# Regrouped adaLN panels, a later input load, moved context steps and paired heads in a two-model kernel on one core

## The chip, the core and the metric

The kernel runs on one core of a Trainium2 chip, in one launch. The metric is the device time of the whole program in microseconds (us). All data is fp32; a fp32 matmul appears in the trace as two TensorE records.

## What is computed

Two small models are chained on 256 tokens of width 1024. The first has two blocks with adaptive layer norm (adaLN), each with a mixture of 32 experts; the second has two layers with a second stream of 256 context tokens, whose input does not depend on the first model. Cut to what matters:

```python
for l in range(2):                                    # first model
    sh1, sc1, g1, sh2, sc2, g2 = split(silu(c) @ w_ada[l] + b_ada[l])
    u = x * (1 + sc1) + sh1
    mix = even_mixer(u) if l == 0 else odd_mixer(u)   # 0: stick-breaking (8 heads of 64) and retention
    x = layer_norm(alpha * x + (1 + g1) * mix)        # 1: differential attention
    u = x * (1 + sc2) + sh2
    x = layer_norm(alpha * x + (1 + g2) * moe(u))     # 32 experts, 2 per token:
                                                      # (silu(xb @ w1[e]) * (xb @ w3[e])) @ w2[e]
h, hc = x, ctx                                        # second model; its adaLN is of c_2 and c_ctx_2
for i in range(2):
    a, ac = modulate(h, ...), modulate(hc, ...)
    y, yc = swa(a, ac) if i == 0 else neighborhood(a, ac)  # 16 heads of 64, keys: own and context
    h = h + gt1 * y;  h = h + gt2 * swiglu(modulate(h, ...))
    if i == 0:
        hc = hc + gt1c * yc;  hc = hc + gt2c * swiglu(modulate(hc, ...))
```

In the first layer of the second model, query heads share four key and value heads; its scores are masked to a window, those of the second layer have a bias table per head. Every query also sees all 256 context keys.

## The kernel before, in words

**Weights and the ring.** The run is one pass over some 670 MB of weights. Nearly all come in loads of 1 MB (1024 KB, 1.0486 MB) through `ring`, 12 slots in SBUF. Python code (L430 to 590) writes the order of the work by hand with `job(...)`, `ada_jobs(...)`, `ctx_jobs(...)` and `expert_jobs(...)`; the same calls append to `loads`. SyncE's queue runs through `loads` in that order (the loop at L744): load n waits until load n-12, the one that had its slot, is released, and so does everything behind it. A load is released by the TensorE tile that read it last; a load for context steps by the last of the steps that share it (`clast`), an expert load by the end of its phase. Expert loads (issued at L695) pick their expert from a table that the routing computes at run time, so the first of a layer waits for the routing (`info_done`), and all that stand behind it wait too.

**Start and even mixer (TensorE at L950).** ScalarE's own DMA queue issues, one behind the other, `cols`, `const` (0.86 MB by its shape), `x` and `first` (tables of the first mixer; 1 MB each) at L1708. The adaLN weights of the four conditionings are panels of two loads each (`ada(L, g0, g1)`, 16 records a panel, 1.9 us), 12 panels to a layer; the first four are needed before `x` can be modulated into `u`. Then seven projections even.0 to even.6 follow (14 us each, two loads each; two of them in another orientation), with one adaLN panel behind each and from even.3 on two, and the rest of the panels between the parts of the stick-breaking and retention heads. The output projection out0.0 ends the stage.

**Context steps.** All work of the context stream is cut into steps (`context_steps`, L105): q, k, v projections, heads, output, gate, up, down, and keys and values of the second layer. A projection step has 16 records and takes some 3.5 us of TensorE. A 1 MB load serves two such steps (gate n and gate n+1 share one, q and k likewise; a down load serves two down steps). `CTX_PLAN` and `MOE_PLAN` (L75) say how many steps stand at which point of the main stream: after a layer norm (`ln0a`, `ln0b`), in the routing (`route0a`, `route0b`), and in an expert pass at nine places, "g" (after the gather), after the phases 0 to 3, "t" (after the transposes), after phases 4 and 5, and "s" (after the scatter):

```python
CTX_PLAN = {"even": 2, "ln0a": 2, "route0a": 2, "route0b": 3, "ln0b": 2, "ln1a": 2, "route1a": 2, "route1b": 3}
MOE_PLAN = (("111212111",) * 6 + ("211000000",),
            ("111111111", "000101010", "111111111", "000101010", "111111111", "000101010", "111111111", "332000000"))
```

TensorE, ScalarE and VectorE each run their part of a step where `ctx(point)` stands in their own program.

**Experts (TensorE at L1139).** A pass takes four experts (24 loads) or, in three passes of layer 1, one or two (6 or 12 loads): a gather of token blocks by matmul (32 records), four phases gate and up, two phases down with four loads each, a scatter. Layer 0 has seven passes and one left-over pass or more, whose experts are read at run time; layer 1 has eight passes and left-over ones.

**Attention of the second model (TensorE at L1246, VectorE at L2312).** Iteration n makes the scores of head n for both query halves (tiles aS), the transposes of the probabilities of head n-2 (aT), and every second n the output product of a pair (aO). Head n lies in partitions 0 to 63 or 64 to 127 by its parity, and so do the operands of its score products, 64 rows of the array:

```python
d, kv = n % 2, n // 4
at = slice(64 * d, 64 * d + 64)
for qb in range(2):
    one_tile(T(f"aS{L}.{n}", qb), lambda o: [
        (o[:, 0:S], q[:, P * qb:P * qb + P], own),
        (o[:, S:2 * S], q[:, P * qb:P * qb + P], far)])
```

VectorE subtracts the row maxima (`shift`) and scales by the sums (`norm`), ScalarE takes the exponentials and moves the transposes. `SEQ` (L593) is the order of (head, half).

## Time and profile before

| | |
|---|---|
| median of 3 runs | 2567.42 us (2562.49 to 2575.24) |
| profiled execution, its own time | 2564.78 us |
| its span | 2563.0 us |
| TensorE (PE) busy | 2256.5 us, 88% of the span |
| VectorE (DVE) busy | 753.7 us, 29% |
| ScalarE (ACT) busy | 456.2 us, 18% |
| mean granted clock of TensorE | 0.947 of full |
| DMA moved | 675.08 MB, mean 263 GB/s |

The page cuts the span into 40 equal slices of 64 us. A digit is a tenth, 9 being 90% or more:

```profile
PE   5987897898997599888989898679999999889999
...
DVE  1136245322111114561112231147510013761000
...
PEclk9999989999998899899999999888999999899999
DMA  9799379999999946439797999941133443203430
GB/s 398 312 389 366 148 293 421 394 422 415 422 421 412 421 171 250 177 153 421 293 422 294 388 384 404 421 174 66 38 131 140 164 148 126 90 20 131 164 115 17
```

The first four slices are the start and the even mixer, slices 6 to 14 the first expert layer, 15 to 17 the odd mixer, 18 to 26 the second expert layer, and the rest the second model. Where the DMA row stands at 9 and more, the weights come as fast as the queue brings them; from slice 27 on they come faster than they are used. TensorE's digit is high nearly everywhere, also where the transfers set the pace, because its instructions are spread over the stage; so neither row alone says what ends a stage.

### The profile page before, as it was taken

How to read it: one execution, taken by the hardware profiler on the slowest of the kernel's cores; microseconds unless marked ns; L12 is line 12 of the kernel's file. 1: busy time of each engine (PE TensorE's matmuls, PEld its weight loads, DVE VectorE, ACT ScalarE, POOL GpSimd, SP SyncE). 2: the span in 40 equal slices, each digit the busy share in tenths (PEclk: the TensorE clock that was granted, in tenths of full speed). 3: DMA queues.
4: the chain of work that ended last, by engine and by line, in shares of the span. 5: the costliest groups of instructions: out<-in, count | busy, mean ns of one | idle time of the engine just before them, and what ended most of it. 6: DMA issues, size and time to landing. Idle time of an engine off the chain costs nothing.

```text
span 2563.0 us, 29352 instructions
## 1 busy us (share of the span) xinstructions
PE 2256.5 (88%) x11792; PEld 1578.4 (62%) x11792; DVE 753.7 (29%) x1897; ACT 456.2 (18%) x1141; POOL 27.8 (1%) x43
## 2 busy tenths in 40 slices
PE   5987897898997599888989898679999999889999
PEld 3654763455664284675555454257688888568888
DVE  1136245322111114561112231147510013761000
ACT  1012113312000022120000221034510011441000
POOL 0000000000000000000000000000000000110000
PEclk9999989999998899899999999888999999899999
DMA  9799379999999946439797999941133443203430
GB/s 398 312 389 366 148 293 421 394 422 415 422 421 412 421 171 250 177 153 421 293 422 294 388 384 404 421 174 66 38 131 140 164 148 126 90 20 131 164 115 17
DMA packets 94052, 675.08 MB, mean 263 GB/s; under 512 B 10832, under 2 KB 10992, under 8 KB 12384
## 3 DMA queue, kind: packets, MB, share of 16 engines
q1 hardware_dynamic: 91296, 664.84, 64.0%
q0 software_dynamic: 2048, 5.21, 0.8%
q10 hardware_dynamic: 576, 3.17, 0.3%
q8 instruction: 95, 1.56, 0.2%
q14 instruction: 37, 0.30, 0.0%
HBM read 672.13 MB, written 1.05 MB: 263 GB/s over the span
## 4 chain that ended last, share of the span: by engine, by line
PE 69%; DMA 16%; DVE 10%; ACT 2%; issue 2%; SPq 1%; DVEq 0%; ACTq 0%
PE bank L763 68%; DMA ring<-in_moe_w 14%; DMA ring<-in_w_ada 1%; DVE work L2335 1%; DMA ring<-in_even_w_out 1%; DVE tiny L2323 1%; DVE work L1860 1%; DVE scratch L1860 1%; ACT work L1384 1%; DVE work L2346 1%; PE bank L1269 1%; ACT u L1384 1%; ACT res L1384 1%; ACT scratch L1384 0%; SPq L695 0%
## 5 line engine op out<-in xcount | busy, mean ns | idle before, releaser
L763 PE MATMUL bank<-u,ring 128*128 128x256 f32 x2912 | 651.6, 386 | 33.7 <-ACT u L1384 22.1
L763 PEld LDWEIGHTS bank<-u,ring 128*128 128x128 f32 x2912 | 562.8, 194 | 122.2 <-issue 32.7
L763 PE MATMUL bank<-ring,work 128*32 128x512 f32 (+2 forms) x2880 | 411.2, 658 | 117.3 <-DMA ring<-in_moe_w 105.5
L763 PEld LDWEIGHTS bank<-ring,work 128*32 128x32 f32 (+2 forms) x2880 | 119.6, 123 | 363.8 <-issue 358.8
L763 PE MATMUL bank<-scratch,ring 128*128 128x256 f32 x1120 | 256.3, 383 | 0.3 <-issue 0.3
L1384 ACT ACTIVATE work<-bank 128x256 f32<-128x256 f32 (+2 forms) x144 | 70.1, 487 | 1028.5 <-PE bank L763 797.9
L763 PEld LDWEIGHTS bank<-scratch,ring 128*128 128x128 f32 x1120 | 209.6, 191 | 56.6 <-issue 28.9
L763 PE MATMUL bank<-work 128*128 128x128 f32 (+4 forms) x1120 | 206.4, 339 | 23.8 <-ACT work L1384 8.0
L763 PEld LDWEIGHTS bank<-work 128*128 128x128 f32 (+2 forms) x1120 | 166.5, 199 | 59.3 <-issue 23.2
L763 PE MATMUL bank<-work,ring 128*128 128x256 f32 x704 | 152.4, 379 | 2.6 <-DVE work L2369 2.6
L763 PEld LDWEIGHTS bank<-work,ring 128*128 128x128 f32 x704 | 133.6, 190 | 21.4 <-issue 3.3
L763 PE MATMUL bank<-ring,condrep 128*32 128x512 f32 x768 | 97.8, 643 | 31.6 <-DMA ring<-in_w_ada 27.8
L1860 DVE RECIPROCAL scratch<-scratch 128x256 f32<-128x256 f32 (+1 forms) x41 | 89.4, 2181 | 69.4 <-ACT scratch L1384 69.4
L2369 DVE TENSOR_TENSOR work<-work,bank 128x256 f32<-128x256 f32 x44 | 18.5, 421 | 286.2 <-PE bank L763 286.2
L763 PE MATMUL bank<-ring,u 128*128 128x512 f32 (+1 forms) x224 | 91.0, 563 | 0.0
L763 PE MATMUL bank<-chid,ring 128*128 128x256 f32 x352 | 80.6, 382 | 1.3 <-DVE chid L1826 1.3
L2230 DVE TENSOR_TENSOR work<-work,bank 128x512 f32<-128x512 f32 x17 | 11.7, 688 | 236.8 <-PE bank L763 236.8
L763 PEld LDWEIGHTS bank<-ring,condrep 128*32 128x32 f32 x768 | 23.2, 114 | 89.9 <-issue 88.9
L763 PEld LDWEIGHTS bank<-chid,ring 128*128 128x128 f32 x352 | 65.6, 190 | 18.6 <-issue 8.5
L2276 DVE SCALAR_TENSOR_TENSOR res<-bank,mod,res 128x256 f32<-128x256 f32 x32 | 14.7, 484 | 197.9 <-PE bank L763 197.9
L763 PEld LDWEIGHTS bank<-ring,u 128*128 128x128 f32 x224 | 42.4, 190 | 45.3 <-issue 44.2
L1742 DVE STREAM_TRANSPOSE adaT<-bank 128x512 f32<-128x512 f32 x48 | 34.3, 714 | 109.8 <-PE bank L763 109.4
(240 smaller groups left out, 1707.2 us busy)
## 6 DMA issues: line engine op xcount, KB each, us to landing
ring<-in_moe_w SPq DMA_DIRECT2D x360, 1024.0 KB, 16.1
ring<-in_w_ada SPq DMA_DIRECT2D x96, 1024.0 KB, 11.2
ring<-in_w_gate_up SPq DMA_DIRECT2D x44, 1024.0 KB, 6.9
ring<-in_w_down SPq DMA_DIRECT2D x23, 1024.0 KB, 5.0
ring<-in_ctx_gate_up SPq DMA_DIRECT2D x22, 1024.0 KB, 14.2
ring<-in_even_w_in SPq DMA_DIRECT2D x14, 1024.0 KB, 11.0
ring<-in_odd_w_in SPq DMA_DIRECT2D x12, 1024.0 KB, 20.1
ring<-in_na_w_qkv SPq DMA_DIRECT2D x12, 1024.0 KB, 4.9
```

Of the source, the lines that this page charges most:

```text
L763: return pe.matmul(o, l, r, start=start, stop=stop, skip_group_check=True)
L1269: r = pe.transpose(o[:, P * kb:P * kb + P], z[:, P * kb:P * kb + P], ident)
L1384: return act.activation(o, i, func, **kw)
L1742: dve.transpose(adaT[:, :], B(t)[:, :]).then_inc(moved[bank_of[t]], 1)
L1860: step(dve.reciprocal(v, v))
L2230: tt(hid, sil, bank[3][:, :], ALU.mult).then_inc(m["hidden"], 1)
L2276: stt(x[:, k], B(t)[:, 0:S], mod[:, L, gate + k, 0:1], x[:, k], ALU.mult, ALU.add).then_inc(moved[bank_of[t]], 1)
L2323: step(dve.tensor_reduce(sm[:, 0:1], B(tS)[:, S:2 * S], AX_X, ALU.max))
L2335: step(dve.tensor_tensor_reduce(out=z[:, 0:S], in0=B(tS)[:, 0:S], in1=bias, scale=1.0, scalar=sm[:, 0:1], op0=ALU.add, op1=ALU.max, accum_ ...
L2346: ts(z, z, sm[:, 11:12], None, ALU.mult).then_inc(soft_p, 1)
L2369: tt(hidden[:, n], hidden[:, n], B(t)[:, 0:S], ALU.mult).then_inc(moved[bank_of[t]], 1)
```

## The change

Five things are altered.

1. At the start, ScalarE issues `const` and `x` only after the eighth load of the ring has landed, and `first` after it has modulated the input; `x` gets a semaphore of its own, and TensorE and VectorE wait for `first` where its tables are used.
2. The adaLN panels stand in other groups: the fifth ahead of even.0, then two of layer 0 behind each of even.0 to even.2 and the last behind even.3, two of layer 1 behind each of even.4 to even.6, and the rest of layers 1 and 2 at other places among the heads.
3. The context steps are spread in another way: four instead of three at `route0b` and `route1b`, four instead of two at `ln0b` (where ScalarE and VectorE now do their part after the next modulation), and new ones, four at `ln1b` and two at `rms2a`. The expert passes have 69 steps in layer 0 (70 before) and 44 in layer 1 (53 before).
4. `CTX_AHEAD` puts two context loads (qkv 4 and 5) and three (gate_up 17 and 18, the first down load of the next group) in `loads` ahead of the expert loads of the layers.
5. In the attention of the second model an iteration makes the scores of heads 2m and 2m+1 for one query half. The four products alternate between partitions 0 to 63 and 64 to 127 and between two banks. The order of tiles, `SEQ` and GpSimd's waits for the bias tables follow it.

The diff, cut to its core:

```diff
@@ -72,9 +72,11 @@
 
-CTX_PLAN = {"even": 2, "ln0a": 2, "route0a": 2, "route0b": 3, "ln0b": 2, "ln1a": 2, "route1a": 2, "route1b": 3}
-MOE_PLAN = (("111212111",) * 6 + ("211000000",),
-    ("111111111", "000101010", "111111111", "000101010", "111111111", "000101010", "111111111", "332000000"))
+CTX_PLAN = {"even": 2, "ln0a": 2, "route0a": 2, "route0b": 4, "ln0b": 4, "ln1a": 2, "route1a": 2, "route1b": 4,
+    "ln1b": 4, "rms2a": 2}
+CTX_AHEAD = {"route0b": 2, "route1b": 3}
+MOE_PLAN = (("221212010",) + ("111212111",) * 5 + ("111000000",),
+    ("222111000", "000100000", "111111111", "000100000", "111111111", "000100000", "111111111", "221000000"))
...
@@ -455,6 +457,13 @@
             clast[key] = ctile[kind, i]
+    for kind, i in todo:
+        key, src = context_sources(kind, i)
+        if CTX_AHEAD.get(point[0], 0) <= sum(k in cslot and k not in clast for k in cslot):
+            break
+        if key and key not in cslot:
+            cslot[key] = len(loads)
+            new_load(src, ("context", key))
...
@@ -480,32 +489,38 @@
 job("adafin0a", 1)
+ada_jobs(0, 4, 5)
 for g in range(7):
     job(f"even.{g}", 2 if g in (2, 5) else 4, panel(a["even_w_in"][0], g))
-    ada_jobs(0, 4 + g, 5 + g)
-    if g >= 3:
-        ada_jobs(1, g - 3, g - 2)
-ada_jobs(0, 11, 12)
-job("adafin0b", 1)
-for b in range(2):
-    job(f"sbS{b}", 4)
-    ada_jobs(1, 4 + 3 * b, 6 + 3 * b)
-    job(f"sbR{b}", 4)
-    ada_jobs(1, 6 + 3 * b, 7 + 3 * b)
-    job(f"sbO{b}", 2)
-job("retS", 4)
+    if g < 4:
+        ada_jobs(0, 5 + 2 * g, min(7 + 2 * g, 12))
+    elif g == 4:
+        job("adafin0b", 1)
+    if g >= 4:
+        ada_jobs(1, 2 * g - 8, 2 * g - 6)
+job("sbS0", 4)
+ada_jobs(1, 6, 9)
+job("sbR0", 4)
+ada_jobs(1, 9, 10)
+job("sbO0", 2)
+job("sbS1", 4)
 ada_jobs(1, 10, 12)
 job("adafin1a", 1)
 job("adafin1b", 1)
+job("sbR1", 4)
+ada_jobs(2, 0, 1)
+job("sbO1", 2)
+job("retS", 4)
+ada_jobs(2, 1, 3)
 job("retO", 4)
-ada_jobs(2, 0, 2)
+ada_jobs(2, 3, 5)
 job("retM", 2)
-ada_jobs(2, 2, 4)
 job("adafin2a", 1)
+ada_jobs(2, 5, 7)
 job("retV", 2)
-ada_jobs(2, 4, 8)
+ada_jobs(2, 7, 9)
 ctx_jobs("even")
-ada_jobs(2, 8, 12)
+ada_jobs(2, 9, 12)
...
@@ -552,13 +567,14 @@
 ctx_jobs("ln1b")
-assert not todo, todo
-x_banks(ALL_BANKS)
 for L in (2, 3):
...
     if L == 2:
+        ctx_jobs("rms2a")
+        assert not todo, todo
+        x_banks(ALL_BANKS)
...
@@ -590,7 +606,7 @@
 
-SEQ = [(h, qb) for h in range(HQ) for qb in range(2)]
+SEQ = [(2 * (n // 2) + d, n % 2) for n in range(HQ) for d in range(2)]
...
@@ -951,7 +967,7 @@
         ada_sums(0, "a")
-        pe.wait_ge(first_in, 32)
+        ada(0, 4, 5)
...
@@ -960,11 +976,12 @@
                 project(f"even.{g}", rhs, S)
-            ada(0, 4 + g, 5 + g)
-            if g >= 3:
-                ada(1, g - 3, g - 2)
-        ada(0, 11, 12)
-        ada_sums(0, "b")
+            if g < 4:
+                ada(0, 5 + 2 * g, min(7 + 2 * g, 12))
+            elif g == 4:
+                ada_sums(0, "b")
+            if g >= 4:
+                ada(1, 2 * g - 8, 2 * g - 6)
...
@@ -973,14 +990,21 @@
                     (o[:, 256:384], sk[:, h // 2, P:S], sq_pad[:, h, P:S])])
-            ada(1, 4 + 3 * b, 6 + 3 * b)
+            ada(1, 6 + 4 * b, 9 + 3 * b)
+            if b:
+                ada_sums(1, "a")
+                ada_sums(1, "b")
             pe.wait_ge(sb_sp, b + 1)
+            pe.wait_ge(first_in, 16)
             for i in range(4):
...
                     (o[:, 256:384], after, sb_l[:, i, 256:384])])
-            ada(1, 6 + 3 * b, 7 + 3 * b)
+            if b:
+                ada(2, 0, 1)
+            else:
+                ada(1, 9, 10)
...
@@ -1246,24 +1268,29 @@
             if n < HQ:
-                d, kv = n % 2, n // 4
-                at = slice(64 * d, 64 * d + 64)
-                if L == 2:
-                    q = wq[at, n // 2]
-                    own = (kx if kv % 2 == d else kxs)[at, kv // 2]
-                    far = (ck if kv % 2 == d else cks)[at, kv // 2]
-                else:
-                    q, own, far = nq[at, n // 2], nk[at, n // 2], nkc[at, n // 2]
-                for qb in range(2):
-                    one_tile(T(f"aS{L}.{n}", qb), lambda o: [
-                        (o[:, 0:S], q[:, P * qb:P * qb + P], own),
-                        (o[:, S:2 * S], q[:, P * qb:P * qb + P], far)])
+                tiles = [T(f"aS{L}.{n}", d) for d in range(2)]
+                for t in tiles:
+                    open_tile(t)
+                for far in range(2):
+                    for d in range(2):
+                        at = slice(64 * d, 64 * d + 64)
+                        kv = n // 2 // 2
+                        if L == 2:
+                            q = wq[at, n // 2]
+                            own, kept = (kx, ck) if kv % 2 == d else (kxs, cks)
+                            keys = (kept if far else own)[at, kv // 2]
+                        else:
+                            q, keys = nq[at, n // 2], (nkc if far else nk)[at, n // 2]
+                        qb = n % 2
+                        r = mm(B(tiles[d])[:, S * far:S * far + S], q[:, P * qb:P * qb + P], keys)
+                        if far:
+                            r.then_inc(filled[bank_of[tiles[d]]], 1)
             if 2 <= n < HQ + 2:
                 v = n - 2
-                for qb in range(2):
-                    t = T(f"aT{L}.{v}", qb)
-                    z = zbuf[L][(2 * v + qb) % 6]
-                    pe.wait_ge(soft_p, SB0[L] + 2 * v + qb + 1)
+                for d in range(2):
+                    t = T(f"aT{L}.{v}", d)
+                    z = zbuf[L][(2 * v + d) % 6]
+                    pe.wait_ge(soft_p, SB0[L] + 2 * v + d + 1)
...
@@ -1311,6 +1338,8 @@
         rms_sums(f"rms{L}a", RMS_N[L][0])
+        if L == 2:
+            ctx("rms2a")
...
@@ -1510,6 +1539,7 @@
         modulate(0, 0)
+        act.dma_start(first, a["first"]).then_inc(first_in, 16)
...
@@ -1536,6 +1566,7 @@
         modulate(1, 0)
+        ctx("ln0b")
...
@@ -1706,13 +1739,13 @@
     act.dma_start(cols[:, :], a["cols"]).then_inc(cols_in, 16)
-    act.dma_start(const[:, :], a["const"]).then_inc(const_in, 16)
-    act.dma_start(x, a["x"]).then_inc(first_in, 16)
-    act.dma_start(first, a["first"]).then_inc(first_in, 16)
     act.wait_ge(cols_in, 16)
     f(cond[:, :], cols[:, 0:24], ACT.Silu).then_inc(cond_done, 1)
+    act.wait_ge(loaded[loads[7][0]], 16)
+    act.dma_start(const[:, :], a["const"]).then_inc(const_in, 16)
+    act.dma_start(x, a["x"]).then_inc(x_in, 16)
     act.wait_ge(const_in, 16)
-    act.wait_ge(first_in, 32)
+    act.wait_ge(x_in, 16)
...
@@ -2314,11 +2352,11 @@
             h, qb = SEQ[q]
-            tS = T(f"aS{L}.{h}", qb)
+            tS = T(f"aS{L}.{q // 2}", q % 2)
             sm = tiny[:, 16 + 16 * (q % 4):32 + 16 * (q % 4)]
             z = zbuf[L][q % 6]
             if q >= 6:
-                is_filled(dve, T(f"aT{L}.{h - 3}", qb))
+                is_filled(dve, T(f"aT{L}.{q // 2 - 3}", q % 2))
...
@@ -2400,7 +2438,7 @@
         if h >= 4:
-            pool.wait_ge(soft_z, SB0[3] + 2 * (h - 4) + 2)
+            pool.wait_ge(soft_z, SB0[3] + 4 * ((h - 4) // 2) + 3 + h % 2)
```

## Rows read from the trace of the kernel before

**Rows 1.** Stretches of the run and their engines, PEclk, DMA share, GB/s

```profile
core 0: us, PE busy (x) PEld busy (x) DVE busy (x) ACT busy (x) POOL busy (x), PEclk, DMA share, GB/s
39.00:165.00 126.00, 124.29 (x593) 81.90 (x594) 17.46 (x50) 11.02 (x21) 0.00 (x0) 0.98 0.86 349
165.00:241.00 76.00, 60.55 (x409) 33.62 (x411) 42.56 (x83) 20.85 (x25) 1.10 (x2) 0.89 0.92 375
374.00:886.00 512.00, 429.53 (x2673) 245.59 (x2673) 127.00 (x290) 82.25 (x199) 0.00 (x0) 0.93 1.00 416
1166.00:1665.00 499.00, 426.39 (x2398) 251.02 (x2391) 100.60 (x205) 55.15 (x112) 0.00 (x0) 0.95 0.92 377
```

**Rows 2.** DMA issues: count, KB each, median us from issue to landing

```profile
res<-in_x ACTq DMA_DIRECT2D x1, 1024.0 KB, 15.8
res<-in_first ACTq DMA_DIRECT2D x1, 1024.0 KB, 20.3
```

**Rows 3.** Timeline (start us, us, row, [idle before <-releaser]), PE before output projection

```profile
39.42 16.45 PE L763 MATMUL bank<-u,ring 128*128 128x256 f32 x64 [2.80 <-ACT u L1384]
...
87.45 1.92 PE L763 MATMUL bank<-ring,condrep 128*32 128x512 f32 x16
...
265.99 9.26 PE L763 MATMUL bank<-u,ring 128*128 128x256 f32 x34 [3.16 <-DMA ring<-in_even_w_out]
```

**Rows 4.** One of the stretches in which the DMA engines ran nearly dry

```profile
100.00:105.00 5.00, 5.00 (x32) 3.19 (x34) 0.81 (x2) 0.00 (x0) 0.00 (x0) 1.00 0.15 25
```

**Rows 5.** Timeline, routing and first pass of the first expert layer

```profile
338.75 3.74 SPq L695 DMA_DIRECT2D ring<-in_moe_w  x4
...
351.13 5.60 PE L763 MATMUL bank<-work 128*128 128x128 f32 x32 [1.00 <-ACT work L1384]
...
356.56 3.62 PE L763 MATMUL bank<-scratch,ring 128*128 128x256 f32 x16
...
360.11 3.64 PE L763 MATMUL bank<-ring,work 128*32 128x512 f32 x32
```

**Rows 6.** Timeline, second expert layer: first loads, and the gathers of three passes

```profile
1128.61 3.76 SPq L695 DMA_DIRECT2D ring<-in_moe_w  x4
...
1142.42 5.44 PE L763 MATMUL bank<-work 128*128 128x128 f32 x32 [2.33 <-DVE work L2200]
...
1213.72 3.73 PE L763 MATMUL bank<-work 128*128 128x128 f32 x32
...
1255.99 3.81 PE L763 MATMUL bank<-work 128*128 128x128 f32 x32 [0.87 <-DVE work L2239]
```

**Rows 7.** Timeline, PE around the two layer norms after the expert layers

```profile
903.48 7.07 PE L763 MATMUL bank<-scratch,ring 128*128 128x256 f32 x32
...
912.47 2.83 PE L763 MATMUL bank<-u,ring 128*128 128x256 f32 x12 [1.92 <-ACT u L1384]
...
1678.91 3.69 PE L763 MATMUL bank<-scratch,const 128*128 128x256 f32 x16 [1.13 <-ACT scratch L1384]
...
1701.23 9.78 PE L763 MATMUL bank<-u,ring 128*128 128x256 f32 x32 [6.43 <-ACT u L1384]
```

**Rows 8.** A stretch inside the attention of the third layer

```profile
1767.30:1771.00 3.70, 3.70 (x10) 2.49 (x9) 3.39 (x15) 3.45 (x12) 0.00 (x0) 0.50 0.00 0
```

**Rows 9.** Timeline of PE there: transposes, output product, score products

```profile
1792.18 1.09 PE L1269 MATMUL bank<-const,work 128*128 128x128 f32 x8
...
1797.70 1.03 PE L763 MATMUL bank<-scratch,ckv 128*64 128x256 f32 x8
...
1799.20 0.59 PE L763 MATMUL bank<-ckv,work 64*128 64x256 f32 x2
1799.63 0.59 PE L763 MATMUL bank<-work 64*128 64x256 f32 x2
```

**Rows 10.** Chain that ended last: start us, us, what; DVE two heads apart

```profile
1787.19 0.42 DVE u L1780
...
1795.66 0.42 DVE u L1780
```

More of the change, by code:

```diff
@@ L1610, in experts @@
                 layer_norm(f"ln{l}b", 2, l)
-                ctx(f"ln{l}b")
+                if l:
+                    ctx("ln1b")
             def rms(L, half, name):
@@ L1696, in second @@
                 if L == 2:
+                    ctx("rms2a")
                     head_norms(2)
@@ L1894, in even @@
                 dve.wait_ge(const_in, 16)
-                dve.wait_ge(first_in, 32)
+                dve.wait_ge(x_in, 16)
                 modulate(0, 0)
-                ada(0, 4, 5)
+                ada(0, 4, 7)
                 for i in range(4):
                     copy_tile(T("even.1", i), sk[:, i], S)
-                ada(0, 5, 6)
+                ada(0, 7, 9)
                 for i in range(2):
                     copy_tile(T("even.2", i), sv[:, i], 512)
-                ada(0, 6, 7)
+                ada(0, 9, 11)
                 for i in range(4):
                     copy_tile(T("even.3", i), rq[:, i], S)
-                for g in range(4):
-                    ada(0, 7 + g, 8 + g)
-                    ada(1, g, g + 1)
                 ada(0, 11, 12)
                 ada_sums(0, "b")
+                ada(1, 0, 6)
                 for b in range(2):
@@ L1921, in even @@
                     stt(sb_l, sb_t, -2.0, sb_z, ALU.mult, ALU.add).then_inc(sb_d, 1)
-                    ada(1, 4 + 3 * b, 6 + 3 * b)
+                    ada(1, 6 + 4 * b, 9 + 3 * b)
+                    if b:
+                        dve.tensor_copy(condrep[:, :, 0:16], cond[:, 8:16].unsqueeze(2).broadcast_to([P, KT, 16]))
+                        dve.tensor_copy(condrep[:, :, 16:32], cond[:, 16:24].unsqueeze(2).broadcast_to([P, KT, 16]))\
+                           .then_inc(condrep_done, 1)
+                        ada_sums(1, "a")
+                        ada_sums(1, "b")
                     dve.wait_ge(sb_e, b + 1)
@@ L1931, in even @@
                     dve.tensor_copy(tiny[:, 90:91], tiny[:, 91:92]).then_inc(sb_a, 1)
-                    ada(1, 6 + 3 * b, 7 + 3 * b)
+                    if b:
+                        ada(2, 0, 1)
+                    else:
+                        ada(1, 9, 10)
+                dve.wait_ge(first_in, 16)
                 for h in range(4):
@@ L1972, in odd @@
                 modulate(1, 0)
+                ctx("ln0b")
                 tt(tiny[:, 0:2], C("lam", 0, 2), C("lam", 2, 2), ALU.mult).then_inc(lam_p, 1)
@@ L2254, in experts @@
                 layer_norm(f"ln{l}b", 2, l)
-                ctx(f"ln{l}b")
+                if l:
+                    ctx("ln1b")
             def rms(L, half, name):
```

33 lines of the change are left out of this document (13 added, 20 removed).

## The prediction

> **What bounds the kernel now.** I read the stretches of the run first, by their DMA share. In the first expert layer the DMA engines are never idle (share 1.00, 416 GB/s) though TensorE is busy 429.5 of 512 us: transfers end that stage. In the second they are idle 0.08 x 499 = 40 us, in the start and the even mixer 0.14 x 126 + 0.08 x 76 = 23.7 us [rows 1]. So a load of 1.0486 MB costs 1.0486 / 0.416 = 2.52 us of stage time where the queue is never blocked, and every us in which the queue is blocked by a held slot counts too. The idle time at the start is not lack of work: while the projections run, all 12 slots are full, and a stretch of 5 us shows 0.15 of the DMA rate [rows 4]; yet the output projection at the stage's end waits 3.16 us for its weights [rows 3]. Idle early, late at the end: that can be won. In the attention of the second model no transfer waits; there the chain runs through VectorE, 8.47 us from one copy of a finished pair of heads to the next, 4.23 us a head [rows 10].
>
> **The change, part by part.**
>
> *Start and even mixer.* Before, `x` and `first` cross with the first ring loads and take 15.8 and 20.3 us to land [rows 2]; the first projection starts at 39.42 [rows 3]. After, the first eight loads cross alone: with 4.9 us before the first load moves (my estimate; no row has it), 4.9 + 8 x 2.52 = 25. Then `const` (0.86 MB) and `x` share the engines with the ring at about half rate, 4 and 5 us: `x` is there at about 35 to 36, `u` 2 to 3 us later, so even.0 starts at about 39, as before. The panel put ahead of it (1.92 us [rows 3]) fills the gap. The gain is behind it: with two panels, four loads, used per projection in place of two, the ring moves on sooner. The 88 loads up to the first out0 panel and some 4.6 MB beside them take 88 x 2.52 + 4.6 / 0.416 + 4.9 = 238 us without a stop; the wait ends at 265.99, so 28 us are stops, 23.7 of them in the stretches above. Going through the order by hand with 14 to 16 us a projection I find 14 us left (even.0 still holds the ring, and even.4 to even.6 each need as long as six loads). That gives 252 for out0.0, with TensorE's own work not far below. **-14 us**; ends -22 (half the remaining stops go as well) and -8 (TensorE's order among the heads, with its new waits, takes the rest). The new wait for `first` stands ahead of the sbR products, far behind its landing; nothing queues on it.
>
> *First expert layer.* Two loads fewer in the bound stage: -5.0. Against it stand the two loads ahead. SyncE starts the layer at 338.75 [rows 5]. The ring has 12 slots and two of them now hold k and v weights, read after the gather and after the first phase. Ten expert loads go out at once and are in after 25 us, at about 365; the eleventh waits for step k1, the twelfth for v1, at about 372 by the gather of 5.60, steps of 3.62 and phases of 3.64 us [rows 5]. That is 5 to 8 us of idle DMA in a stage that has none. In return TensorE has four steps in front of the block table where it had three, and gathers at a higher clock (3.8 us in [rows 6] against 5.60 in [rows 5]), which a transfer-bound stage does not pay out. Sum **0**; ends -5 (k and v are through before the ten loads are) and +4.
>
> *Four steps at ln0b.* Two take 7.07 us from 903.48, and the odd projection starts at 912.47 after a wait of 1.92 us for ScalarE [rows 7]. Four take 14.1, to 917.6; the wait is under them. **+5.1**; ends +4 and +7.
>
> *Second expert layer.* 53 steps become 44, seven loads fewer: 7 x 2.52 = -17.6 us, if the queue runs. Three slots now hold gate_up 17, 18 and a down load. The queue starts at 1128.61 and the gather at 1142.42 [rows 6]; nine loads are in after 23 us, the tenth waits for step up13, the eleventh for up15 (after phase 0), the twelfth for down13 (after phase 1). With two steps of 3.62 at each of these places and phases of 3.64 [rows 5], the DMA engines stand 17 to 20 us in pass 0. Pass 1 gathers at 1213.72 now [rows 6]; I get about 10 us later. Second hold: the load that gate16 and gate17 share is read at "t" of pass 0 and again in the third phase of pass 1, so its slot is kept over a whole scatter and gather, and the load twelve behind it waits some 24 us, against some 18 at the same place now, where the pass of one expert holds the ring between gathers at 1213.72 and 1255.99 [rows 6]. Together stops grow by 25: **+7.4**; ends -7 (stops as before but for the thin-pass slot, less 17.6) and +12. Routing is 2 us sooner for the gather, since VectorE has no step of its own there (2.33 us waited now [rows 6]), but transfers decide.
>
> *ln1b and rms2a.* The LN sums end at 1678.91 + 3.69 = 1682.6 [rows 7]. Four steps take 14.1, to 1696.7; ScalarE's squares for the next norm queue behind its copies of these steps, the sums come at about 1697.6 to 1701.3, the two rms2a steps of 7.1 lie beside the root and the modulation, and the projection starts at 1708.4 in place of 1701.23. It starts at full clock, which saves some 2.3 of its 9.78 us (32 records at the 2.83 / 12 of the odd start are 7.5), since TensorE no longer stands 6.43 us idle ahead of it [rows 7]. 7.2 - 2.3 = **+4.9**; ends +2 and +10 (the half clock stays, and the sums come later).
>
> *Attention, both layers.* The score products are two rows of two records, 0.43 us apart [rows 9], 1.72 us a head; in a product on 64 columns, eight records take 1.03 [rows 9], so column halves pack already. Here two row halves would run side by side. No row shows such a pair: the ends are no overlap, 0, and full overlap, 0.86 us a head. Steady heads don't gain: VectorE sets 4.23 us [rows 10], TensorE needs 1.09 + 1.72 + 1.0 = 3.8 [rows 9]. Only heads 2 to 5, run at half clock, 0.50 of 2.4 GHz with TensorE never idle [rows 8], are TensorE's, and lose some 4.4 us to the steady pace, which halved score time gives back. **-4.4 a layer, -8.8**; ends -10 and 0. If tile modes must be switched the product drains. The Trainium skill's page "TensorEngine Tiling (Array Packing)", under Key Properties, states that different tiles run loads and matmuls in parallel, and that a change of mode drains the array; no run here shows either for row halves.
>
> **Sum.** -14 + 0 + 5.1 + 7.4 + 4.9 - 8.8 = **-5.4 us**. The profiled execution, 2564.78, becomes 2559.4; it stands 2.6 below the median of the runs, 2567.42, and my number is against the latter: **2562.0**. A measurement of this kernel can tell about 0.5%, 12.8 us: faster is below 2554.6, slower above 2580.3.
>
> **Rivals.**
> *F, the loads ahead pay.* If k, v and the gate_up slots come free before the other loads are in, there is no stop and the fewer loads count in full: layer 0 -5 in place of 0, layer 1 at its lower end of -7 in place of +7.4: -5.4 - 5 - 14.4, about -25 in all, 2543. For it: TensorE has slack (429 of 512 us [rows 1]), and steps may be read sooner than I place them. Against it: the hold follows from the order and from durations of rows.
> *N, row halves don't overlap.* +8.8 on the sum: +3.4, about 2571. For it: the 0.43 us spacing of the present order shows nothing of pairs.
> *S, the held ring slots.* One mechanism, at the thin pass of layer 1: each expert pass behind a late one gathers late, and the transfers lost there are not made up. From 20 us of stops beyond my 25 it decides: -5.4 + 20 = +14.6, 2582, slower. For it: the 40 us idle there now [rows 1] come from held slots already. Against it: thin passes are shorter by two steps (7 us each), which returns slots.
> *C, the clock.* TensorE ran a gap-free stretch at 0.50 in [rows 8]. With scores halved it would be busy 1.09 + 0.86 + 1.0 = 2.95 of 4.23 us. If the clock then stayed at half in both attentions, a head would need 5.9 us: +1.6 for 16 heads twice, about +50, less the heads that are so already and the sum's 8.8: some +33, about 2600. The steady heads ran at full clock with 3.8 of 4.23. The Trainium skill's page "TensorE: Matmul & The Clock Gate", in its section on the HAM clock gate, states that throttled is the default and that activity releases it.
>
> **Chances.** My sum 0.50, F 0.24, N 0.12, S 0.09, C 0.05. The forecast's own range is 2550 to 2574 (its parts' ends, not all at once), so part of it is faster by over 0.5%: 0.12 of its 0.50, and nearly all of F, 0.22: faster 0.34. Slower: S, most of C: 0.12. Same: the rest, 0.54. For 8 in 10 the range reaches from F's centre to beyond N: 2543 to 2577; left out are half of F's lower side, S and C.
>
> **What would show it.** Right: out0.0 starts near 252; DMA idle 5 to 8 us between 360 and 380; pass 1 of layer 1 gathers 8 to 10 us later against its own stage start, and the DMA share of that stage falls to about 0.86; odd.0 starts 5 us later and in2 7 us later after their norms; four score products of a pair span about 0.9 us, while the steady pace stays 8.47 per two heads. Wrong: DMA share at 1.00 through both first passes (F), score products still 0.43 apart (N), a granted clock of 0.5 throughout the attention (C), or out0.0 after 262, which would take the largest term away.

## The result and the profile after

The changed kernel takes 2578.78 us (median of 13 runs, 2573.94 to 2583.09) against 2566.8 us for the kernel before (13 runs): ratio 1.0047, 95% interval 1.0036 to 1.0057. That is 12 us slower by the ratio, where a gain of 5 us (2562.0) was forecast and the range ended at 2577: outside the range, and a loss in place of a gain. The loss itself is clear of the noise, small as it is. Its profiled execution has a span of 2577.7 us, 14.7 more than the one before.

The stretches of the changed kernel, as in [rows 1], with the columns named there; five shorter ones follow that the text comes back to, and two inside the attention:

```profile
core 0: us, PE busy (x) PEld busy (x) DVE busy (x) ACT busy (x) POOL busy (x), PEclk, DMA share, GB/s
39.00:165.00 126.00, 124.35 (x605) 80.95 (x602) 19.12 (x56) 12.63 (x24) 0.00 (x0) 0.98 0.93 381
165.00:241.00 76.00, 59.69 (x416) 33.52 (x415) 49.26 (x95) 20.85 (x25) 1.09 (x2) 0.92 0.98 402
374.00:886.00 512.00, 424.19 (x2614) 240.46 (x2614) 124.71 (x295) 75.68 (x189) 0.00 (x0) 0.92 0.99 410
1166.00:1665.00 499.00, 398.36 (x2196) 221.94 (x2192) 98.27 (x200) 50.18 (x103) 0.00 (x0) 0.93 0.87 359
348.00:364.00 16.00, 16.00 (x106) 9.40 (x105) 0.00 (x0) 2.95 (x5) 0.00 (x0) 1.00 0.56 215
1148.00:1166.00 18.00, 18.00 (x111) 11.69 (x113) 2.31 (x7) 0.00 (x0) 0.00 (x0) 1.00 0.51 191
1166.00:1184.00 18.00, 12.99 (x68) 7.51 (x64) 1.75 (x4) 0.60 (x1) 0.00 (x0) 0.83 0.59 231
1220.00:1250.00 30.00, 22.15 (x96) 14.12 (x88) 7.25 (x18) 3.08 (x7) 0.00 (x0) 0.99 0.14 51
1346.31:1451.22 104.91, 88.79 (x457) 51.09 (x456) 22.10 (x53) 9.91 (x24) 0.00 (x0) 0.95 0.75 306
1801.00:1803.00 2.00, 2.00 (x19) 1.16 (x18) 1.83 (x10) 1.38 (x6) 0.00 (x0) 1.00 0.00 0
1819.50:1822.90 3.40, 3.40 (x17) 1.59 (x16) 3.02 (x14) 2.87 (x12) 0.00 (x0) 0.51 0.02 5
```

The start moves more bytes than before (381 and 402 GB/s for 349 and 375), the second expert layer fewer (0.87 for 0.92). In both expert layers there are stretches (348 to 364, 1148 to 1166) in which TensorE works without a gap and the DMA engines stand idle for 0.44 and 0.49 of the time: the sign of a ring whose next slot is held.

The timeline of TensorE in the changed kernel gives the marks of each stage: the output projection of the even mixer, the first gather of each expert layer, the odd projection, the sums of the layer norm behind each expert layer (the products on `res,const`), the first score product of the second model. (253.04 and 911.85 are shown up to the end of the stretch that was read, so their lengths say nothing.)

```profile
253.04 9.33 PE L779 MATMUL bank<-u,ring 128*128 128x256 f32 x42
...
337.79 5.44 PE L779 MATMUL bank<-work 128*128 128x128 f32 x32 [2.39 <-DVE work L2237]
...
888.24 5.13 PE L779 MATMUL bank<-res,const 128*128 128x256 f32 x16 [4.12 <-issue]
...
911.85 48.51 PE L779 MATMUL bank<-u,ring 128*128 128x256 f32 x224
...
1140.69 5.27 PE L779 MATMUL bank<-work 128*128 128x128 f32 x32 [2.39 <-DVE work L2237]
...
1686.39 5.38 PE L779 MATMUL bank<-res,const 128*128 128x256 f32 x16 [4.12 <-issue]
...
1775.06 1.11 PE L779 MATMUL bank<-work 64*128 64x256 f32 x4 [0.69 <-ACT work L1413]
```

Those of the kernel before that were not shown ahead of the prediction:

```profile
893.44 5.38 PE L763 MATMUL bank<-res,const 128*128 128x256 f32 x16 [4.12 <-issue]
...
1672.40 5.38 PE L763 MATMUL bank<-res,const 128*128 128x256 f32 x16 [4.12 <-issue]
...
1757.29 0.79 PE L763 MATMUL bank<-work 64*128 64x256 f32 x2 [0.69 <-ACT work L1384]
```

Taking mark from mark, after against before, the lead grows and is lost again:

| up to | after minus before, us | change in the stage | forecast |
|---|---|---|---|
| out0.0 (265.99 before [rows 3]) | -13.0 | -13.0 | -14 |
| first gather, layer 0 (351.13 [rows 5]) | -13.3 | -0.4 | |
| layer norm after layer 0 | -5.2 | +8.1 | 0 |
| odd projection (912.47 [rows 7]) | -0.6 | +4.6 | +5.1 |
| first gather, layer 1 (1142.42 [rows 6]) | -1.7 | -1.1 | |
| layer norm after layer 1 | +14.0 | +15.7 | +7.4 |
| first scores of the second model | +17.8 | +3.8 | +4.9 |
| end | +14.7 | -3.1 | -8.8 |

Three terms are off, all of them the same way: both expert layers (16 us together) and the attention (6 us).

A mark from one profiled execution has a spread of its own. From the first gather to the layer norm of layer 0 it is 542.3 us here before the change, and 538.3 to 543.2 in the eight traces of this study whose plan of that layer is the one before; with the changed plan and the loads ahead it is 550.5 and 548.4. So a difference of some 5 us in one expert layer of one trace shows nothing by itself.

### The profile page after: what moved, and what is told of

It is laid out like the page before. It is cut to its first block, busy times and chain, and to the rows that moved or that the text cites. A ratio compares the mean times of both kernels' runs of the same rounds, so it can differ in the third digit from the quotient of the medians.

```text
span 2577.7 us, 29375 instructions
## 1 busy us (share of the span) xinstructions
PE 2240.2 (87%) x11792; PEld 1554.1 (60%) x11792; DVE 753.4 (29%) x1897; ACT 452.9 (18%) x1139; POOL 26.8 (1%) x43
## 3 DMA queue, kind: packets, MB, share of 16 engines
q8 instruction: 95, 1.56, 0.2%
## 4 chain that ended last, share of the span: by engine, by line
PE 67%; DMA 18%; DVE 10%; issue 2%; ACT 2%; SPq 1%; DVEq 0%; ACTq 0%
PE bank L779 66%; DMA ring<-in_moe_w 17%; DVE work L2373 1%; DVE tiny L2361 1%; DMA ring<-in_w_ada 1%; DVE scratch L1893 1%; ACT work L1413 1%; DVE work L1893 1%; SPq L711 1%; DVE work L2384 1%; DMA res<-in_x 1%; ACT scratch L1413 0%; DVE tiny L2383 0%; ACT u L1413 0%; PE bank L927 0%
## 5 line engine op out<-in xcount | busy, mean ns | idle before, releaser
L779 PE MATMUL bank<-u,ring 128*128 128x256 f32 x2912 | 646.6, 384 | 21.6 <-ACT u L1413 12.6
L779 PE MATMUL bank<-ring,work 128*32 128x512 f32 (+2 forms) x2880 | 429.8, 682 | 150.6 <-DMA ring<-in_moe_w 139.7
L779 PE MATMUL bank<-work 128*128 128x128 f32 (+4 forms) x1120 | 186.4, 340 | 26.3 <-ACT work L1413 8.7
L779 PEld LDWEIGHTS bank<-work 128*128 128x128 f32 (+2 forms) x1120 | 152.9, 198 | 63.1 <-issue 26.3
L1296 PE MATMUL bank<-const,work 128*128 128x128 f32 x256 | 43.1, 306 | 35.0 <-DVE work L2384 28.5
L2314 DVE SCALAR_TENSOR_TENSOR res<-bank,mod,res 128x256 f32<-128x256 f32 x32 | 14.7, 483 | 197.9 <-PE bank L779 197.9
L2271 DVE COPY work<-bank 128x512 f32<-128x512 f32 x17 | 11.7, 691 | 198.8 <-PE bank L779 198.8
```

Of the source, the lines that this page charges most:

```text
L779: return pe.matmul(o, l, r, start=start, stop=stop, skip_group_check=True)
L1296: r = pe.transpose(o[:, P * kb:P * kb + P], z[:, P * kb:P * kb + P], ident)
L2271: dve.tensor_copy(ysb[:, 512:1024], bank[0][:, :]).then_inc(m["y_by_dve"], 1)
L2314: stt(x[:, k], B(t)[:, 0:S], mod[:, L, gate + k, 0:1], x[:, k], ALU.mult, ALU.add).then_inc(moved[bank_of[t]], 1)
```

## The experiments

All times are medians; a ratio is to runs of the kernel before on the same chip at the same time, and "less" or "more" without a name is against that kernel, by the ratio. The experiments were timed in three groups: `start_only`, `att_only`, `plan_only` and `no_ahead`; `start_att`, `start_att_fill`, `no_split` and `ahead_one`; `mix`, `mix_fill` and `late_tail`. Within a group medians are compared; across groups the ratios count, since the median of the kernel before moved by up to 3 us from one to the next.

### The change in three parts

`start_only` is the kernel before with items 1 and 2 of the change:

```diff
-act.dma_start(x, a["x"]).then_inc(first_in, 16)
-act.dma_start(first, a["first"]).then_inc(first_in, 16)
+act.wait_ge(loaded[loads[7][0]], 16)
...
+act.dma_start(x, a["x"]).then_inc(x_in, 16)
...
-            ada(0, 4 + g, 5 + g)
+            if g < 4:
+                ada(0, 5 + 2 * g, min(7 + 2 * g, 12))
```

> The kernel before with the start alone changed (later const and x, regrouped adaLN panels). Theory A (terms add): out0.0 starts near 253 us as in the changed kernel, and nothing behind it gives that back, since the first expert layer starts with it: 13 us faster, about 2554. Theory B (the gain is absorbed): the transfers of the expert layer do not start earlier in effect, 0 to 5 us faster, 2562 to 2567.

2552.77 us, ratio 0.9943 (0.9925 to 0.9961), 14.6 us less. In its trace out0.0 starts at 251.38, the layer norm after layer 1 comes 11.9 us earlier than before and the end 11.2: theory A, the gain is not absorbed.

`att_only` has item 5 alone:

```diff
-SEQ = [(h, qb) for h in range(HQ) for qb in range(2)]
+SEQ = [(2 * (n // 2) + d, n % 2) for n in range(HQ) for d in range(2)]
...
+    for far in range(2):
+        for d in range(2):
```

> The kernel before with paired heads alone. Theory A: the halved score time gives some 4.6 us back to heads 2 to 5 of each attention, and a lower clock behind the emptier TensorE takes most of it back, as in the changed kernel: 3 us faster, 2564, with copies of a finished pair 8.5 us apart at full clock and 9.9 us apart where the output products run at half. Theory B: the lower clock came from what stands ahead of the attention in the changed kernel; then pairs stay 8.47 us apart and it is 9 us faster, 2558.

2563.36 us (2555.45 to 2571.43), ratio 0.9981 (0.9967 to 0.9994). Some 5 us less, between the 3 and the 9 that were set against each other. Its timeline decides: with nothing changed ahead of the attention, in six of the eight pairs of the first attention an output product takes 1.8 us or more in place of 1.03 (in two of eight before), and two copies of finished pairs, at 1777.07 and 1787.02, are 9.95 us apart. The lower clock comes with the paired heads and not from what stands ahead of them: theory A. The trace also gives a sharper price than the median: from the first scores of the second model to the end it takes 802.7 us, before 805.7. That is 3.0 less, as in the whole change (3.1); the rest of this trace's lead was there at the first scores already, where nothing differs.

`plan_only` has items 3 and 4:

```diff
-CTX_PLAN = {"even": 2, "ln0a": 2, "route0a": 2, "route0b": 3, "ln0b": 2, "ln1a": 2, "route1a": 2, "route1b": 3}
+CTX_PLAN = {"even": 2, "ln0a": 2, "route0a": 2, "route0b": 4, "ln0b": 4, "ln1a": 2, "route1a": 2, "route1b": 4,
+            "ln1b": 4, "rms2a": 2}
+CTX_AHEAD = {"route0b": 2, "route1b": 3}
...
```

> The kernel before with the moved context steps and the loads ahead alone. Theory A (terms add): the stages from the first gather to the attention lose 8 + 5 - 1 + 16 + 4 = 31 us, about 2598. Theory B (part of the loss comes from the layer starting earlier): 15 to 20 us slower, 2582 to 2587.

2589.93 us, ratio 1.0090 (1.0071 to 1.0109): 23 us slower in ratio, just beyond theory B's 15 to 20 and short of theory A's 31. With -14.6 and -5 it comes to +3.5, where the whole change shows +12. The 8.5 us between them are just outside what the four intervals allow together (8 us), so the parts add up only roughly; with theory A's +31 it would be +11. The trace of `plan_only` has +6.1 for the first expert layer and +13.4 for the second, where the whole change has +8.1 and +15.7: part of the loss may come from the layers starting earlier, but that isn't shown. What is certain is that this part alone turns the change into a loss.

### The loads ahead

`no_ahead` and `ahead_one` are the changed kernel with

```diff
-CTX_AHEAD = {"route0b": 2, "route1b": 3}
+CTX_AHEAD = {}
```

and with one load at each place in place of none.

> The changed kernel with no context loads ahead of the expert loads. Theory A (held slots): the 7 us of idle DMA in the first pass of layer 0 and some 16 us in that of layer 1 go, some of it paid back by context loads that come later: 10 to 15 us faster than the changed kernel, 2564 to 2569. Theory B (the plan of steps is the cause, not the order of loads): the idle time moves to other passes, 0 to 4 us, 2575 to 2579.

> The changed kernel with one context load ahead in each layer in place of two and three. Theory A (slots held by loads that are read late): the one load is read right after the first gather, 28 us after the queue starts, about when the other eleven loads are in, so nothing is held: 2556 to 2561, as without any. Theory B (any load ahead delays the experts' loads): a third to a half of the 20 us, 2565 to 2570.

`no_ahead`: 2558.38 us, ratio 0.9959 (0.9945 to 0.9973). `ahead_one`: 2558.29 us, ratio 0.9961 (0.9945 to 0.9977). So the two and three loads ahead cost 20 us by the medians and 23 by the ratios, more than either theory had (17 in the two traces), and one load ahead costs nothing that can be measured. It isn't the order as such; it is a slot taken by a load that is read late. The same stretches without loads ahead, and the first of them with one:

```profile
348.00:364.00 16.00, 16.00 (x106) 9.34 (x104) 0.00 (x0) 2.96 (x5) 0.00 (x0) 1.00 1.01 422
1148.00:1166.00 18.00, 18.00 (x114) 10.93 (x113) 1.26 (x3) 0.60 (x1) 0.00 (x0) 1.00 1.01 422
1166.00:1184.00 18.00, 18.00 (x114) 10.91 (x113) 3.32 (x7) 0.00 (x0) 0.00 (x0) 1.00 1.01 421
1200.00:1230.00 30.00, 24.71 (x112) 14.84 (x104) 7.26 (x18) 3.08 (x7) 0.00 (x0) 0.97 0.13 45
```

```profile
348.00:364.00 16.00, 16.00 (x105) 9.17 (x104) 0.00 (x0) 2.99 (x6) 0.00 (x0) 1.00 1.01 422
```

At 0.56, 0.51 and 0.59 in the changed kernel, these are 16 x 0.44 = 7 us and 18 x 0.49 + 18 x 0.41 = 16 us of standing transfers, and both are gone when k and v in layer 0 and the two gate_up loads and the down load in layer 1 don't stand ahead. With them ahead, each is read some steps after the ring ran full. The layer norm after layer 0 comes at 881.50 in place of 888.24, that after layer 1 at 1669.59 in place of 1686.39: 7 us from the one, 10 from the other. In layer 1 16 us of idle time are gone and 10 appear in the time, for the stop of the next section stays.

### The slot that is held across two passes

In `no_ahead`, DMA stands at 0.13 from 1200 to 1230 (above), and behind it TensorE waits for an expert load (that it is one of those that were shut out is inferred from the order):

```profile
1233.05 6.75 PE L779 MATMUL bank<-ring,work 128*128 128x512 f32 x8 [5.10 <-DMA ring<-in_moe_w]
```

gate16 is read in the first pass of layer 1, gate17, from the same load, in the third phase of the second. `no_split` puts both at the second place:

```diff
-            ("222111000", "000100000", "111111111", ...
+            ("222110000", "000200000", "111111111", ...
```

> The changed kernel without loads ahead, and with step gate16 moved from the first pass of layer 1 to the third phase of the second, beside gate17, so that the load that both read is not kept over the scatter and the gather. Theory A (that slot holds the ring): the some 26 us of nearly idle DMA between 1200 and 1230 shrink to 15 or less, 5 to 10 us faster than without this edit, 2548 to 2553. Theory B (the pass with one expert is idle anyway, the ring being full): the same 2558.

2552.63 us, ratio 0.9942 (0.9926 to 0.9957): 5.8 us less than `no_ahead` by the medians, 4.4 by the ratios, whose intervals overlap. The stretch in its windows:

```profile
1200.00:1230.00 30.00, 26.96 (x110) 18.34 (x111) 7.13 (x18) 3.33 (x8) 0.00 (x0) 1.00 1.00 410
```

0.13 becomes 1.00: that one slot held the ring is shown. What it is worth is less sure. Idle time comes back later, in the pass behind the third gather (15 us from 1246 to 1320, where `no_ahead` has 2 in the same pass), so over the whole layer it falls by 10 us. The layer norm comes at 1659.81, 9.8 earlier, but the profiled run of `no_ahead` was its slowest; the medians say 6 and the ratios 4. Why the idle time comes back there was not tested.

### The plan of layer 0

`mix` is `no_split` with the passes of layer 0 and `route0b` of the kernel before.

```diff
-"route0b": 4
+"route0b": 3
...
-MOE_PLAN = (("221212010",) + ("111212111",) * 5 + ("111000000",),
+MOE_PLAN = (("111212111",) * 6 + ("211000000",),
```

> no_split with the passes of layer 0 and route0b as in the kernel before (70 and 3 steps), the rest of the changed plan kept, no loads ahead. Theory A (the changed plan of layer 0 costs by itself: attention steps of the context, which wait for VectorE, stand where the ring is full): last gather of layer 0 some 4 us earlier, 2548. Theory B (the small difference in layer 0 is noise or only the two loads): the same as no_split, 2552 to 2555.

2547.07 us, ratio 0.9928 (0.9914 to 0.9943): 5.6 us less than `no_split`'s median, 3.6 by the ratios, whose intervals overlap. The traces are firmer. From the first to the last gather of layer 0 the three kernels with the changed plan and at most one load ahead take 481.5 to 482.0 us, the eight with the plan before 474.8 to 480.9 (477 in the middle). So the changed plan of layer 0 costs some 4 us, theory A. Windows of `no_split`, then of `mix`:

```profile
476.00:508.00 32.00, 25.11 (x183) 10.52 (x185) 11.41 (x41) 11.42 (x30) 0.00 (x0) 0.95 0.73 297
```

```profile
476.00:508.00 32.00, 27.23 (x196) 11.36 (x194) 11.99 (x42) 12.05 (x34) 0.00 (x0) 0.95 0.94 388
```

The changed kernel has 0.70 here, the kernel before 0.92: 7 us of transfers are lost in a stage that is otherwise at 1.00. The idle time lies around the gather of the third pass, which the attention steps of the context surround. They end in transposes that wait for VectorE. Five such waits of 2.38 or 2.39 us stand in both `mix` and the kernel before, so the waits as such are not new; but in `no_split` the one between the gather and the first phase is longer (`no_split`, then `mix`):

```profile
481.88 1.08 PE L927 MATMUL bank<-const,scratch 128*128 128x128 f32 x4 [3.91 <-DVE scratch L1813]
```

```profile
486.01 0.63 PE L927 MATMUL bank<-const,scratch 128*128 128x128 f32 x4 [2.38 <-DVE scratch L1813]
```

From the end of the last phase of one pass to the first phase of the next, between which no expert load of a phase is read, TensorE needs 19.7 us in `no_split` (463.2 to 482.9) and 16.3 in `mix` (462.6 to 478.9), and the full ring waits that much longer. That the new places of the head steps cause this is my reading of the timelines; `mix` takes back the whole plan of the layer and `route0b`, not these steps alone. I had not gone past pass 0 in this layer.

### Fewer loads in the last passes

`late_tail` is start and paired heads with the plan of the kernel before, but the last passes of layer 1 have six steps fewer, which stand at `ln1b` (four) and `rms2a` (two). `start_att` is the start and the paired heads alone. (`late_tail` also keeps from the changed kernel that ScalarE and VectorE do their part of `ln0b` after the next modulation.)

```diff
-"111111111", "000101010", "111111111", "332000000"))
+"111111111", "000010000", "111111111", "220000000"))
...
+            "ln1b": 4, "rms2a": 2}
```

> The start and the paired heads together, with the context steps and the order of loads of the kernel before. Theory A (the gains add): 14.6 + 5 us below the kernel before, about 2549. Theory B (part of the gains needs the changed plan, or is noise): 2553 to 2558.

> Start and paired heads, the plan of the kernel before but for six steps taken out of the last passes of layer 1 and put at ln1b (four) and rms2a (two). Theory A (the last passes are bound by transfers at share 1.00, three loads are 7.5 us, the six steps cost 3.5 behind): 4 us faster than start_att, 2545 to 2551. Theory B (the time returns as a TensorE or ring wait): no faster than start_att, 2551 to 2557.

`start_att` takes 2555.26 us (2542.63 to 2556.8), ratio 0.9947 (0.9930 to 0.9965); `late_tail` 2552.25 us, ratio 0.9939 (0.9925 to 0.9952). They can't be told apart in time. From the first gather to the layer norm of layer 1 `late_tail` takes 532.3 us, the five kernels with the full plan of that layer 529.8 to 533.1: three loads less and not shorter. The trace says where their 7.5 us went. `start_att`, then `late_tail`:

```profile
1442.00:1478.00 36.00, 35.13 (x205) 21.60 (x206) 11.37 (x20) 8.96 (x15) 0.00 (x0) 1.00 0.79 313
1490.00:1530.00 40.00, 34.40 (x200) 22.22 (x193) 16.63 (x24) 6.43 (x13) 0.00 (x0) 0.96 1.01 421
```

```profile
1442.00:1478.00 36.00, 33.08 (x198) 20.27 (x197) 7.32 (x19) 5.08 (x11) 0.00 (x0) 1.00 0.63 259
1490.00:1530.00 40.00, 31.49 (x168) 16.97 (x169) 11.44 (x9) 4.35 (x8) 0.00 (x0) 0.87 1.01 421
```

The later stretch is bound by transfers in both; the earlier one, with the ring full, stands 0.16 x 36 = 6 us longer. A transfer that is taken out of a pass with a full ring ahead of it is paid only if the ring can be refilled sooner, and here it wasn't. That is theory B.

### The clock in the attention

Score products do overlap. The eight records of one iteration and the transposes behind them, in the timeline of the changed kernel, and an output product at either pace:

```profile
1794.60 0.70 PE L779 MATMUL bank<-work 64*128 64x256 f32 x4
1795.14 0.60 PE L779 MATMUL bank<-ckv,work 64*128 64x256 f32 x4
1795.67 1.09 PE L1296 MATMUL bank<-const,work 128*128 128x128 f32 x8
...
1801.94 1.03 PE L779 MATMUL bank<-scratch,ckv 128*64 128x256 f32 x8
...
1821.08 1.93 PE L779 MATMUL bank<-scratch,ckv 128*64 128x256 f32 x8
```

The eight records take 1.07 us up to the transposes; before, two records took 0.43 [rows 9] and eight 1.72 or more. Four records on both row halves take 0.54 or 0.53 where they touch work on the whole array, and 0.43 to 0.44 where groups of them follow each other (in `start_att_fill`), as two did before. So row halves run side by side. The Trainium skill's page "TensorEngine Tiling (Array Packing)" (Key Properties) states that different tiles can run matmuls in parallel, and this trace agrees. But the copies of finished pairs, in the chain of the changed kernel, are

```profile
1799.91 0.41 DVE u L1813
1808.37 0.43 DVE u L1813
1818.32 0.42 DVE u L1813
1828.26 0.43 DVE u L1813
1838.22 0.41 DVE u L1813
```

8.46, 9.95, 9.94 and 9.96 us apart. The first is the pace of [rows 10], at a granted clock of 1.00 in the windows above (2.4 GHz). In the others the output products run at 0.51 (1.2 GHz), the next score products come late and VectorE waits for them. Between the pairs TensorE stands idle for its turn with VectorE: busy 46.87 of 60 us in this kernel's attention (1785 to 1845), in idle gaps of 1.4 to 1.6 and 0.55 us. The Trainium skill's page "TensorE: Matmul & The Clock Gate" (the HAM clock gate) gives the same direction: throttled by default, released by activity.

`start_att_fill` gives TensorE its emptiness back as work: from iteration 6 on, each score product is made twice into the same bank.

```diff
-for far in range(2):
+for rep, far in [(i, j) for i in range(1 + (n >= 6)) for j in range(2)]:
```

> The same, and from iteration 6 of both attentions on each score product is made twice into the same bank; the result is the same, TensorE has 0.86 us more to do per head. Theory A (TensorE's emptiness lowers its clock, and the half-clock output products make a pair 9.9 us): granted clock 1.0 from there on, pairs 8.5 to 8.9 us apart throughout, 3 to 8 us faster than without the doubled products. Theory B (the pace of 9.9 us has another cause): no faster, or slower by up to 0.86 us x 26 = 22 us.

2549.72 us (2546.52 to 2552.16), ratio 0.9928 (0.9912 to 0.9943), 5.5 us less than `start_att` by the medians. Its window over the pairs of the first attention, and its copies of finished pairs:

```profile
1760.00:1812.00 52.00, 44.14 (x348) 30.92 (x348) 45.51 (x192) 39.99 (x140) 0.00 (x0) 1.00 0.00 1
```

```profile
1773.17 0.43 DVE u L1798
1782.34 0.43 DVE u L1798
```

The clock is 1.00 in this window, and a pair takes 9.17 us: less than 9.95, more than 8.46. Each repeated product has its own price. The medians alone don't prove the gain: the runs of the two kernels overlap, and so do the intervals. The traces settle it better, because from the first scores on nothing but the attention differs between these kernels:

| traces | first scores to the end, us | first to last copy of a finished pair, first and second attention |
|---|---|---|
| `before`, `start_only`, `plan_only` | 805.4 to 806.1 | 50.6; 52.8 to 52.9 |
| changed kernel, `att_only`, `no_ahead`, `no_split`, `ahead_one`, `mix`, `late_tail` | 802.3 to 803.2 | 55.1 to 56.8; 52.6 to 54.1 |
| `start_att` | 798.9 | 50.6; 53.6 |
| `start_att_fill`, `mix_fill` | 799.4 and 800.0 | 53.7 and 54.2; 52.8 and 51.2 |

In all seven kernels of the second row, three or four pairs of the first attention stand 9.6 us or more from the next; in the first row and in `start_att` none does, and in the filled kernels none is above 9.2. So the fill keeps the clock up in the first attention of both traces that have it, and is worth 2 to 4 us against an unfilled kernel that loses its clock. But `start_att` stands in the way of a simple rule. In its one profiled run, the fastest of its six, TensorE has the same idle gaps (1.56 and 0.55 us) as in the changed kernel, its pairs are 8.46 or 8.47 us apart, and its clock stays up:

```profile
1763.00:1810.00 47.00, 33.92 (x259) 22.11 (x256) 42.24 (x181) 36.80 (x131) 0.85 (x2) 1.00 0.00 1
```

An emptier TensorE can lose its clock; it doesn't lose it every time, and against this run the fill gains nothing. What decides from run to run is open.

`mix_fill` is the same edit on `mix`.

> The same with the score products made twice from iteration 6 on. Theory A (the clock decides the pace of pairs): granted clock 1.0 in both attentions, 3 to 6 us faster than mix. Theory B (doubled products cost as much as the clock gives, since pairs at 9.2 us in the first attention stand between 8.5 and 9.9): within 2 us of mix.

2545.7 us, ratio 0.9921 (0.9907 to 0.9935), 1.4 us less than `mix`: what theory B said, but the intervals overlap and A's 3 us is not excluded; from the first scores on, the two traces are 3.2 us apart. It is the fastest kernel of the study, 21 us ahead of the kernel before and 33 ahead of the changed one; `mix`, without repeated products, is not distinguishable from it.

## Why the prediction was wrong

*Start: right.* -14 forecast, -13.0 in the trace, 14.6 when made alone. out0.0 starts at 253.04 where 252 was said.

*First expert layer: the failed step.* "Sum 0" took the idle DMA of pass 0 as 5 to 8 us; it is 7, as `no_ahead` shows. The prediction had already rounded these terms down, since -5 and 5 to 8 make 0 to +3. What was missed stands 120 us further on: 7 us more idle DMA at 476 to 508 than before, which `mix` shows to come from the changed plan of the layer and not from the loads ahead. 7 + 7 - 5 for two loads is 9, for the 8.1 measured. The prediction priced the moved steps of layer 0 at nothing beyond their loads and never followed the ring past pass 0; that TensorE takes 3.4 us longer around the third gather, with a longer wait for VectorE in it, is what the traces show there, and which step is at fault stays open.

*Second expert layer: the two stops right, the credit for seven loads wrong.* The stage from the first load to the layer norm moves 543.8 us x 380 GB/s = 207 MB before and 558.0 x 357 = 199 MB after, by these windows of the two kernels, before and after:

```profile
1128.60:1672.40 543.80, 459.96 (x2587) 275.41 (x2586) 123.09 (x276) 61.09 (x123) 0.00 (x0) 0.95 0.93 380
```

```profile
1128.40:1686.40 558.00, 444.15 (x2460) 253.35 (x2458) 121.60 (x272) 54.27 (x113) 0.00 (x0) 0.93 0.87 357
```

At the 421 GB/s of an unblocked stretch that is 491 and 473 us, seven loads less, as forecast. The stops are the rest, 53 and 85: they grow by 32 where I said 25, and 32 less 18 is the 14 us by which this stretch is longer. Where the 32 lie is seen beside two windows of the kernel before:

```profile
1230.00:1270.00 40.00, 38.28 (x185) 26.60 (x184) 9.70 (x23) 3.47 (x8) 0.00 (x0) 1.00 0.60 226
1322.88:1429.15 106.27, 93.96 (x490) 56.86 (x489) 22.86 (x54) 11.09 (x25) 0.00 (x0) 0.95 0.84 337
```

16 are the three loads ahead (forecast: 17 to 20). The hold at the thin pass, forecast at 24 for 18, is 0.86 x 30 = 26 (1220 to 1250) for 0.40 x 40 = 16: +10. Both places were named in the prediction, and its stops there are right within 4 us. Another 9 were not named: from the fourth gather to the sixth, 1346.31 to 1451.22, the DMA engines stand for 0.25 x 105 = 26 us, before for 0.16 x 106 = 17. In that stretch the changed kernel moves 32.1 MB for 35.8, some 3.5 loads less, which at 2.52 us each should save 9 us; it is 1.4 us shorter. So the step that failed is "7 x 2.52 = -17.6 us, if the queue runs": half of the seven loads fall out of this one stretch, whose passes don't wait for transfers all the time, and there a load less is more idle time and hardly any gain. `late_tail` shows the same with three loads.

Rival S had the sign and the size (2582), and I gave it 0.09; its mechanism, 20 us more at the thin pass, is not what happened, where 4 more than forecast were found. F, at 0.24, was the case without holds; `no_ahead`, 2558, has no loads ahead and still falls 15 us short of F's 2543; the hold at the thin pass and the plan of layer 0 remain in it.

*ln0b, ln1b and rms2a: right*, +4.6 for 5.1 and +3.8 for 4.9.

*Attention: half right.* Heads 2 to 5 gained what was said in the first attention: from the first scores to the first copy 29.9 us before and 24.9 after. In the second it is 3.7, 29.7 and 26.0. The step that failed is "Steady heads don't gain" taken as don't lose. Rival C had the mechanism and asked for too much: not all pairs at half clock and not +33, but three pairs of the first attention at +1.5 each, which takes 4.5 back, and two of the second at +0.7 (9.57 for 8.88). What is left is 0.6 and 2.4, the 3.1 measured for 8.8. The prediction also took one pace for both attentions; the steady pairs of the second stood 8.88 us apart before the change, not 8.47.

## What to carry to other kernels

In a ring of slots filled in order, a load belongs where its slot is free again before the ring comes round: twelve slots filled in 30 us leave 30 us between issue and last reading, and steps that share a load belong in one pass. In this kernel cutting transfers paid only where the ring wasn't full ahead of them; look at the DMA share pass by pass, not at the stage's mean. And TensorE made emptier can lose its clock: weigh the work saved against the granted clock of what stands next to it.

## What was not expected of the hardware

Making every score product twice, 0.86 us more TensorE work a head, made the attention shorter and not longer: from the first scores to the end 799.4 and 800.0 us in the two filled traces, 802.3 to 803.2 in the seven of paired kernels that lose their clock, at a granted clock of 1.00 in place of a mixture of 1.00 and 0.51. In the whole time this is 5.5 us by one pair of medians (2549.72 for 2555.26) and 1.4 by the other, neither clear of the noise. And two products on the two halves of the array's rows, written to two banks, cost no more than one: eight records in 1.07 us, where the same eight took 1.72 and more in turn. Left open: why the filled pairs take 9.17 us at full clock and not 8.46, and why the profiled run of `start_att` held the full clock in its first attention. That run takes 2542.63 us, 12.6 less than the median of its kernel; of these the attention can explain some 4.
